# Weights, parameters and constants placed at the top of SBUF, the normed activations at the bottom, and a smaller room for descriptors

## What is computed

```python
def reference(...):
    x = first_block(x, ...)
    return second_block(x, ...)

x = x + y                                     # first block: y from gated_deltanet
x = x + squared_relu_mlp(rms_norm(x, norm_mlp[i]), mlp_w_up[i], mlp_w_down[i])
...
x = x + mx[2] * (jnp.concatenate([att_x, hg_x], axis=-1) @ w_out[l])     # second block
x = x + mx[5] * swiglu(modulate(rmsnorm(x, g_norm2[l]), mx[3], mx[4]), w_gu[l], w_down[l])
```

## Time and profile before

| | |
|---|---|
| median of 3 runs | 3102.67 us (3102.61 to 3103.27) |
| the profiled execution, first to last instruction (span) | 3102.1 us |
| the profiled execution's own time | not given apart from its span; the median of the runs is 0.6 us above it |
| TensorE (PE) busy | 2953.6 us, 95% |
| VectorE (DVE), ScalarE (ACT), GpSimd (POOL) busy | 1820.8, 1210.9, 901.7 us |
| TensorE's mean granted clock | 0.987 of full speed |
| bytes moved by DMA | 274 MB, mean 88 GB/s |

### The profile page before, as it was taken

How to read it: one execution, slowest core, us unless ns; L and a number is a source line. 1 busy time by engine, 2 the same in 40 slices (tenths; PEclk the granted TensorE clock), 3 DMA queues, 4 the chain that set the end, 5 groups by cost and what they waited for, 6 DMA issues and landing times.

```text
span 3102.1 us, 37785 instructions
## 1 busy us (share of the span) xinstructions
PE 2953.6 (95%) x14715; PEld 2445.9 (79%) x14715; DVE 1820.8 (59%) x2359; ACT 1210.9 (39%) x1929; POOL 901.7 (29%) x684
## 2 busy tenths in 40 slices
PE   7899999989999999999998999999989999999997
PEld 6688888878788888888876777888878778887886
DVE  7566566564365544333366886554574866666866
ACT  5555555553311112221334776222332444444222
POOL 5333332221000000000302886331331444443423
PEclk9999999999999999999999999999999999999999
DMA  3111111112143333111210001011023144446953
GB/s 128 41 48 48 48 48 48 42 62 102 41 129 110 111 113 102 48 48 54 93 53 21 11 9 49 28 35 35 21 75 149 40 157 150 148 148 239 371 207 122
DMA packets 96833, 274.00 MB, mean 88 GB/s; under 512 B 9232, under 2 KB 31248, under 8 KB 92176
## 3 DMA queue, kind: packets, MB, share of 16 engines
q1 hardware_dynamic: 96656, 271.58, 25.0%
HBM read 208.43 MB, written 60.36 MB: 87 GB/s over the span
## 4 chain that ended last, share of the span: by engine, by line
PE 81%; DVE 10%; ACT 4%; issue 3%; POOL 1%; DMA 1%; SPq 0%; POOLq 0%; DVEq 0%; ACTq 0%
PE ps L663 25%; PE ps L1756 11%; PE ps L3068 11%; PE ps L3729 9%; PE ps L3096 7%; DVE b L3677 2%; PE ps L2659 2%; PE ps L1060 1%; DVE b L652 1%; PE ps L2466 1%; PE ps L2437 1%; PE ps L2465 1%; PE ps L1067 1%; PE ps L2480 1%; PE ps L90 1%
## 5 line engine op out<-in xcount | busy, mean ns | idle before, releaser
L663 PE MATMUL ps<-b 128*128 128x512 f32 x3912 | 1009.6, 403 | 29.7 <-DVE b L652 14.4
L663 PEld LDWEIGHTS ps<-b 128*128 128x128 f32 x3912 | 711.4, 191 | 159.2 <-issue 20.1
L1756 PE MATMUL ps<-b 128*128 128x512 f32 x1536 | 361.7, 396 | 0.6 <-DVE b L1924 0.6
L1756 PEld LDWEIGHTS ps<-b 128*128 128x128 f32 x1536 | 288.0, 188 | 69.5 <-DVE b L1924 1.0
L3729 PE MATMUL ps<-b 128*128 128x512 f32 (+1 forms) x1464 | 326.1, 377 | 6.3 <-ACT b L3788 5.9
L3729 PEld LDWEIGHTS ps<-b 128*128 128x128 f32 x1464 | 253.8, 191 | 55.6 <-issue 10.6
L644 ACT ACTIVATE b<-b 128x1024 fp32r<-128x1024 f32 x138 | 145.2, 1054 | 319.5 <-PE ps L1756 242.3
L3121 ACT ACTIVATE b<-b 128x512 fp32r<-128x512 f32 x232 | 142.3, 615 | 270.9 <-PE ps L3096 106.3
L652 DVE TENSOR_TENSOR b<-b 128x1024 fp32r<-128x1024 f32 x138 | 174.2, 1264 | 107.6 <-ACT b L644 98.5
L3068 PE MATMUL ps<-b 128*128 128x512 f32 x960 | 225.9, 393 | 6.0 <-DVE b L3371 3.8
L3068 PEld LDWEIGHTS ps<-b 128*128 128x128 f32 x960 | 180.5, 189 | 48.3 <-DVE b L3371 7.7
(11 more groups left out here) (372 smaller groups left out, 5011.4 us busy)
## 6 DMA issues: line engine op xcount, KB each, us to landing
inner<-b SPq DMA_DIRECT2D x77, 512.0 KB, 2.6
b<-inner SPq DMA_DIRECT2D x35, 1024.0 KB, 13.5
b<-in_down SPq DMA_DIRECT2D x52, 512.0 KB, 4.3
b<-in_mod SPq DMA_DIRECT2D x96, 256.0 KB, 2.6
b<-scratch SPq DMA_DIRECT2D x46, 512.0 KB, 4.4
b<-in_gu SPq DMA_DIRECT2D x44, 512.0 KB, 4.1
b<-in_dn_in SPq DMA_DIRECT2D x32, 512.0 KB, 4.9
b<-in_up SPq DMA_DIRECT2D x32, 512.0 KB, 3.7
```

The source lines that it names most:

```text
L663: ins = e.matmul(ps[:, c], w, h[:, k, c], start=first and k == 0 and i == 0, stop=last and k == KT - 1 and i == 2)
L1756: ins = e.matmul(ps[:, c], w, u[:, at[k], c], start=k == 0 and p == 0, stop=k == n - 1 and p == 2)
```

## The change

`st`, `params`, `con_t`, `raw`, `whi`, `wlo`, `mod` and the small vectors are allocated from the right, so they lie at the top of the memory, each below the one before. `b_hi` and `b_lo` are then the first tiles on the left, and each stage's tiles follow directly behind them. The room for descriptors, at the bottom, is set to 1024 bytes where it had its default of 16,384; the left side's first free byte is then 1,121. The tiles that were on the right before the change lie below the moved ones. No instruction, wait, size or order is edited.

```diff
     def memory(self):
 
         sb = self.sb
-        self.st = sb([128, 48])
-        self.params = sb([128, NPAR])
-        self.con_t = sb([128, NCON])
-        self.raw = [sb([128, 1024]) for _ in range(RAW)]
-        self.whi = [sb([128, 1024], F32R) for _ in range(SPL)]
-        self.wlo = [sb([128, 1024], F32R) for _ in range(SPL)]
+        top = lambda shape, dt=F32: sb(shape, dt, side="right")
+        self.st = top([128, 48])
+        self.params = top([128, NPAR])
+        self.con_t = top([128, NCON])
+        self.raw = [top([128, 1024]) for _ in range(RAW)]
+        self.whi = [top([128, 1024], F32R) for _ in range(SPL)]
+        self.wlo = [top([128, 1024], F32R) for _ in range(SPL)]
+        self.mod = top([128, 48, 2])
+        self.ax, self.ac, self.a2, self.lb, self.olb = (top([128, 8]) for _ in range(5))
+        self.lbw, self.wfa = top([128, 24]), top([128, 8])
         self.b_hi, self.b_lo = (sb([128, KT, T], F32R) for _ in range(2))
-        self.mod = sb([128, 48, 2])
-        self.ax, self.ac, self.a2, self.lb, self.olb = (sb([128, 8]) for _ in range(5))
-        self.lbw, self.wfa = sb([128, 24]), sb([128, 8])
         self.cw = self.lbw[:, 16:24]
...
-    nc = build(lambda: bacc.Bacc("TRN2", target_bir_lowering=False, num_devices=1), arrays)
+    nc = build(lambda: bacc.Bacc("TRN2", target_bir_lowering=False, num_devices=1, dynamic_dma_scratch_size=1024), arrays)
```

## The result

The changed kernel takes 3131.13 us (median of four, 3127.33 to 3131.52) against 3102.97 for the kernel before: ratio 1.0087, interval 1.0072 to 1.0102. It is slower by 28 us. The profiled execution is the fastest of the four, 3127.33 us with a span of 3125.6, so its gap to the span before (3102.1) is 23.5 us and understates the medians' difference. No instruction was added or moved; L663 of before is L664 here, and so on by one line.

A forecast was written before the change was run, and what follows sets the result against it. TensorE's distance from one matmul to the next bounds the kernel; 24.5 + 6.3 - 1 = +29.8 us on a span of 3102.1 gives 3131.9, median 3132.5, forecast 3132; own range 3119 to 3142, 8 in 10 from 3099 to 3142.

The forecast's parts named there:

- term 1: Long back-to-back runs of L3068, L3096, L663 and L3036 lose agreement: 24.5 us more, bounds 20 to 29.
- term 7: PE's waits for other engines shrink where their work ran beside a slower PE: -1 us, bounds -5 and 0.
- term 2: Groups of 2 to 6 matmuls, mainly early L663 and L3729's 1152, slow by 2.2 ns each: 6.3 us, bounds 0 to 20.
- term 3: L1756's 1536, the 720, the 276 and L3729's 312 differ before and after: 0, bounds -1.4 to +1.4 us.
- term 4: Plain fp32 matmuls over identity or `ones` with stage tiles lose agreement: 0 taken, bounds 0 to 4.5 us.
- Room: Descriptor room cut from 16 KiB to 1 KiB: no transfer is issued from POOL, nothing used it; cost nothing.
- VectorE, ScalarE: L652 and L1924 differ by 39 ns, which would be 5 us of DVE either way, beside PE: 0.
- The signs it named: L663 x192 at 44.8 to 45.0 us, L1756 x96 near 22.4, both L3068 groups near 399 ns, attention still reaching 227.
- Only the moving tile counts: Weights at 32 cost nothing under moving tiles at 0, so slow matmuls are cured: -18.5 us, 3084; chance of faster 0.14.
- No change: TensorE's ports do not meet, and 227 and 234 ns come from something else: 3102.7 us; chance 0.10.

The follow-up runs named there:

- the kernel that agrees by 512: Changed kernel plus three unused tiles, so that weights and all moving tiles have remainder 128 by 512: 3085.64 us, ratio 0.9947.
- the kernel with TensorE alone: Separate kernel computing nothing of the reference: stretches of 96 matmuls, each at one moving-tile offset, no other engine working; 21.76 to 22.72 us per 96.
- the kernels at 0 and at 32: Changed kernel with two unused 32-byte tiles, putting weights and moving tiles all at remainder 0, or all at 32, by 64: 3125.24 and 3125.5 us.

## Why the prediction was right, and where it was not

*The size* was right: +29.8 us forecast, 28.2 between the medians, though its terms were off in both directions, so that the closeness is partly luck. The 3132 of the forecast stand against 3131.1, inside the forecast's own range of 3119 to 3142.

*What bounds the kernel* was right: the distance between matmuls. TensorE's extra 27.6 us of busy time carry the result.

*Long runs* (term 1, 24.5 us, bounds 20 and 29) gave some 19 of busy time. L664 from 748 us on answers to the earlier trace rows:
```profile
L664 PE MATMUL ps<-b 128*128 128x512 f32 x1843 | 434.0, 396 | 5.9 <-DVE b L653 4.4 <-ACT b L1781 1.2 <-DVE b L2170 0.3
```
That is 11.8 us more than the 422.2 before, 10.6 without the five matmuls that the window takes in besides, and L664's 372 of the output projection give 2.0 (90.4 against 88.4): together 12.6, near the forecast's 13.3. L3097 gave 3.7 of 4.5, L3037 0.2 of 0.9 and L3069 2.8 of 5.8. In L3069 the start distance of the "b" pieces did go from 227.1 to 233.3 ns, but their short waits for VectorE shrank: the 48 from 2499.96 us take 11.18 us before (to 2511.14), wait included, and the 48 from 2518.82 take 11.29 after. So part of term 7's gain lies here.

*Short runs* (term 2, 6.3 us, bounds 0 and 20) gave more, some 9. L3730's 1152 are busy 2.7 us more, 2.3 ns each, close to the 2.2 taken. The larger part, L664 ahead of the long stretch, was undersized (us, busy us of L664; before it was 480.36 for x1620):
```profile
0.00:748.20 748.20, 486.80 (x1621) 0.98 0.17 55
```
That is 6.4 us more, 4.0 ns each (3.8 without the one matmul more): over half of the full difference and not a third. About 1 us of it may be chance: the kernel that agrees by 512, where these matmuls are as they were before the change, has 481.62 us for the same 1621. Short runs of L664 feel the addresses more than the prediction took from attention's groups.

*What differs before and after* (term 3, 0 with 1.4 either way): L1757 +1.4 us, at the bound, and L3069's "b,b" 0.0. By 256, `uhi` went from 224 bytes past the weights to 160, and `xs[0]` to `xs[2]` from 160 to 96; in the kernel with TensorE alone these offsets take 22.40, 22.49 and 22.41 us per 96, the same as here (22.40 before and 22.47 to 22.49 now for the down part; 234.2 and 233.3 ns for the 36 of "b,b"). *Small fp32 matmuls* (term 4, 0): L1060's and its twin L1061's 384 are busy 59.1 us both times. *Room* 0: shown by the kernel with the room alone. *VectorE, ScalarE*: the twin of L652 takes 1265 ns after 1264, that of L1924 1226 after 1225. *Given back* (term 7, -1, bounds -5 and 0) was too small: PE's idle time fell by 4.1 us, near the far bound. The kernel with the placement alone has 144.9 us of it, so this is no accident of one execution.

*The signs it named.* L664's 192 take 44.80 us and L1757's 96 22.47 to 22.49, as forecast. Attention's five groups of 160 are busy 318.3 us after 318.5: they kept agreement, by 256 too. L3069's groups are 396 and 399, not both near 399, though their start distances are the same.

*The step that failed* is the reading "about 227 ns when moving tile and weights agree by 64 bytes and 234 when they differ". It was drawn from two facts, 0 over 0 fast and 32 over 32 fast, and in both cases the tiles also agreed by 256. 64 was the finest unit that told the fast rows from the slow ones, and nothing in the rows told it from 128, 256 or (but for `vx`) 512. A hint stood there that a yes or no by 64 does not explain: two slow distances, 233.3 ns at L1756 and 234.2 at L3068, both 32 by 64. The runs put 256 in its place: agreement by 64 alone gives 3125 us, by 256 gives 3087. The forecast survived because the changed layout disagrees by 64 and by 256 alike. It would have been 40 us off for the kernel in which everything lies at a multiple of 64.

*The rivals.* "Only the moving tile counts" (3084) fell with the result and with the kernels at 0 and at 32, which have other remainders and the same time. Its number came true where the prediction did not look for it, in the kernels that agree by 256, since -18.5 us is what curing the old slow matmuls is worth by either reading: 17.2 and 18.7 were measured (agreement by 512 in the new order and in the old). One term of that sum is not borne out: L3730's 312 matmuls of 256 columns are busy 80.4 us with agreement, after 80.2 without, where 3.5 ns each were to be won. "No change" fell too. The rule of the Trainium skill ("SBUF — State Buffer", section "Who interferes with whom") by which TensorE's two read ports are independent and never wait on anyone is not borne out by these traces in that form: with every other engine idle, the same 96 matmuls take 21.76 or 22.72 us by four bytes of address. Where page and measurement differ, the measurement stands. That section's other half, that DMA and the other engines do not slow TensorE's reads, agrees: 226.7 ns is reached beside busy engines and transfers as well as without them.

## What to carry to other kernels

Where many float32r matmuls of 512 columns run back to back, give the weight tile and the moving tile start addresses that differ by a multiple of 256 bytes; here that took three unused tiles, less than 1 KiB together, and is worth 0.5% over the old layout and 1.5% over the changed one. No run here tried other types, and on matmuls of 256 columns no gain showed. A move of tiles in memory that "changes nothing" can undo it, so look at the chain's us per matmul by line after any such move. And when a rule is read from rows, ask for the coarsest unit that fits as well as for the finest, and test between them before a layout is built on either.

## What the runs showed of the hardware

- The distance of 128x512 float32r matmuls, each with its weight load, depends on the difference of the moving tile's and the weights' start address by 256 bytes: 226.7 ns at 0, 228.9 (21.97 us / 96) at 64, 236.7 at 4, 231.6 at 8 and 16, 230.1 at 252, and 233.3 to 234.3 at 32, 48 and from 96 to 240. With difference 0 the remainder does not matter (128, 160 and 320 by 512 gave 3085.6, 3087.1 and 3084.8 us), and with difference 128 it does not either (3125.2 and 3125.5 us with the weights at 0 and at 32 by 64). The cost is there with no other engine at work.
- The profile's mean duration of a matmul shows it too: 389 to 393 ns in the agreeing groups of long runs, 395 to 399 in the others.
- Where tiles lie, at the top or the bottom of the memory, and whether the room for descriptors is 1 or 16 KiB cost nothing that these runs tell from noise (3085.6 against 3084.8 us; ratio 1.0004, 0.9995 to 1.0013).
